# RWKV block-parallel chain: keys by token made by VectorE transposes and a DRAM exchange, and the spread of the block inverse four places down

## The reference, cut to what matters

```python
def rwkv7_scan(r, w, k, v, kk, a, s0):
    def step(s, inp):
        r_t, w_t, k_t, v_t, kk_t, a_t = inp
        s_kk = jnp.einsum('bhvk,bhk->bhv', s, kk_t)
        s = (s * w_t[:, :, None, :] - s_kk[..., None] * (kk_t * a_t)[:, :, None, :]
             + v_t[..., None] * k_t[:, :, None, :])
        return s, jnp.einsum('bhvk,bhk->bhv', s, r_t)
...
    for d, f in enumerate((_ident, _flip)):
        yc_d, s_ctx = rwkv7_scan(f(rc), f(wc), f(kc), f(vc), f(kkc), f(ac), s0)
        yl_d, _ = rwkv7_scan(f(rl), f(wl), f(kl), f(vl), f(kkl), f(al), s_ctx)
```

## Time and profile before

| | |
|---|---|
| median of three runs | 3613.45 us |
| the profiled execution, its own time | 3610.41 us |
| its span | 3608.6 us |
| granted TensorE clock, mean | 0.988 |
| chain of layer 0, first grams to last inverse store | 254.5 to 608.6 us |
| chain of layer 3, likewise | 2970.7 to 3297.3 us |

### The profile page before, as it was taken

One profiled execution on the slowest core, in us unless ns is written; L12 is line 12 of the kernel. 1 busy time (PEld: TensorE's weight loads), 2 busy tenths in 40 slices (PEclk: granted clock), 3 DMA queues, 4 the chain that ended last, 5 costly groups with the idle time before them and its releaser, 6 DMA issues. The chain is left out here.

```text
span 3608.6 us, 74335 instructions
## 1 busy us (share of the span) xinstructions
PE 3447.1 (96%) x28653; PEld 2513.5 (70%) x28653; DVE 2487.9 (69%) x4562; ACT 1156.4 (32%) x2482; POOL 590.4 (16%) x1128
## 2 busy tenths in 40 slices
PE   7998998999999999999999999999999997888999
PEld 2447777688786455555888876678877456777887
DVE  7986665489897657653898954469987956664431
ACT  4035554133202444431233014323310225663210
POOL 1015553000000323320000000000000105553000
PEclk9998999999999999999999999999999998999999
DMA  6641111244353323223444520043434541111454
GB/s 219 207 136 24 21 22 32 74 133 130 118 161 97 105 79 102 82 76 99 129 126 127 162 83 28 25 126 121 136 118 129 170 129 25 25 24 27 134 152 133
DMA packets 584315, 365.07 MB, mean 101 GB/s; under 512 B 126144, under 2 KB 553480, under 8 KB 581928
## 3 DMA queue, kind: packets, MB, share of 16 engines
q1 hardware_dynamic: 557544, 250.40, 25.1%
q0 software_dynamic: 26432, 110.07, 8.7%
HBM read 348.73 MB, written 11.67 MB: 100 GB/s over the span
## 5 line engine op out<-in xcount | busy, mean ns | idle before, releaser
L275 PE MATMUL PS<-H,WR 128*128 128x512 f32 (+1 forms) x1424 | 477.1, 494 | 0.0
L591 DVE SCALAR_TENSOR_TENSOR WORK<-WORK,SC 128x512 f32<-128x512 f32 x616 | 418.3, 746 | 0.7
L275 PEld LDWEIGHTS PS<-H,WR 128*128 128x128 f32 x1424 | 268.0, 190 | 187.3 <-issue 167.2
L2549 PE MATMUL PS<-WORK 64*64 64x64 f32 (+2 forms) x6944 | 361.0, 231 | 29.5 <-ACT BIG L2846 16.6
L571 POOL DMA_DIRECT2D WORK<-in_ada_w_dram x88 | 66.4, 755 | 1857.7 <-DVE WORK L591 839.6
L1474 PE MATMUL PS<-BIG,WR 128*128 128x512 f32 (+1 forms) x944 | 329.4, 503 | 5.2 <-DMA WR<-in_rw_wo_dram 1.7
L2549 PEld LDWEIGHTS PS<-WORK 64*64 64x64 f32 (+1 forms) x6944 | 282.1, 139 | 69.2 <-ACT WORK L2835 23.0
L1474 PEld LDWEIGHTS PS<-BIG,WR 128*128 128x128 f32 x944 | 175.7, 190 | 132.6 <-issue 111.8
L2835 ACT ACTIVATE WORK<-PS 128x64 f32<-128x64 f32 (+3 forms) x528 | 161.4, 326 | 292.0 <-PE PS L2549 286.7
L1012 ACT ACTIVATE WORK<-PS 128x512 f32<-128x512 f32 x252 | 134.7, 541 | 335.6 <-PE PS L945 285.1
L945 PE MATMUL PS<-BIG 128*128 128x256 f32 x984 | 223.9, 380 | 0.0
(11 more groups left out here) (363 smaller groups left out, 6391.0 us busy)
## 6 DMA issues: line engine op xcount, KB each, us to landing
WORK<-in_ada_w_dram POOLq DMA_DIRECT2D x88, 1024.0 KB, 6.3
WR<-in_ffn_w_in_dram SPq DMA_DIRECT2D x220, 256.0 KB, 2.9
BIG<-in_ffn_w_in_dram SPq DMA_DIRECT2D x132, 256.0 KB, 3.4
WR<-in_ffn_w_out_dram SPq DMA_DIRECT2D x106, 256.0 KB, 2.8
WR<-in_ssd_w_in_dram SPq DMA_DIRECT2D x96, 256.0 KB, 2.8
BIG<-scratch_dram POOLq DMA_DIRECT2D x8, 2048.0 KB, 7.9
BIG<-in_ffn_w_out_dram SPq DMA_DIRECT2D x36, 256.0 KB, 3.2
BIG<-in_ada_w_dram SPq DMA_DIRECT2D x4, 2048.0 KB, 15.5
```

The costliest lines, as they stand in the source:

```text
L275: mm = pe.matmul(outs, WR[:, slot, k, 0:m], rhs(k), start=first and k == 0, stop=last and k == nk - 1)
L591: lag(vec.scalar_tensor_tensor(ACC3[:, s_], w, by, ACC3[:, s_], ALU.mult, ALU.add), label)
L2549: return pe.matmul(o, lhs, rhs, start=start, stop=stop)
```

## The change

- `by_token` goes from TensorE and ScalarE (no HB steps) to VectorE as step TB. Per (i, s) there are four transposes of 128x256: of the replacement keys SD (n=1) for d = 0 and 1, then of the removal keys ADS (n=0) for both. VectorE's transpose turns 32x32 blocks within groups of 32 partitions, so the two blocks off the diagonal of each 64x64 land in the wrong partition group.
- BK has the same size and a new layout: [half, direction, which keys, a, 128], where a tells the 32 channels' column block; the four chunks of a half are interleaved, four elements apart. The block a = 1 - b % 2 of each partition group b is exchanged with its neighbour through a DRAM tensor `swapped`: `swap_out`, four DMAs of 32 partitions, a wait, `swap_in`, four DMAs. Each partition has four pieces of 128 elements in one of these.
- SyncE takes the swap of (i-1, 1) between `blocks_in(i, 0)` and `inverse_out(i, 0)`, that of (i, 0) between `blocks_in(i, 1)` and `inverse_out(i, 1)`, and the last one ahead of the output weights.
- `chain_s` waits for the swap at chunks 0 and 4 and takes its weights from BK with a step of four elements.
- TB stands at places 0 to 3 of slot (i, 0) and 0, 1, 4, 6 of slot (i, 1), after the chain's step. E moves from place 1 (s=0) or 2 (s=1) to 5; the levels Z and X from 4 to 14 (s=0) and 5 to 16 (s=1) to 8 to 18. Tile 0's half 0 keeps its places.
- The waits on HB fall away: `vt` for PSUM bank 7; `replacement` on ScalarE now waits for the key grams and for the transposes of the keys.

```diff
@@ -189,6 +189,8 @@
         scratch_stored = sem("scratch_stored")
         first_loaded = sem("first_loaded")
         gram_stored = sem("gram_stored")
+        swap_stored = sem("swap_stored")
+        swap_loaded = sem("swap_loaded")
         blocks_loaded = sem("blocks_loaded")
         inverse_stored = sem("inverse_stored")
         inverse_loaded = sem("inverse_loaded")
@@ -2342,7 +2344,8 @@
         RESET, KF, KK, BS = (work(T) for _ in range(4))
         INV = work(2 * T).rearrange("p (d c f) -> p d c f", d=2, c=NQ)
         TURN = work(T).rearrange("p (d c f) -> p d c f", d=2, c=4)
-        G2, BK, G1R = by_chunk(P), by_chunk(P), by_chunk(Q)
+        G2, G1R = by_chunk(P), by_chunk(Q)
+        BK = work(2 * NQ * P).rearrange("p (s d n a f) -> p s d n a f", s=2, d=2, n=2, a=2)
         sub = lambda: work(4 * Q).rearrange("p (c f) -> p c f", c=4)
         NSALL = work(16 * Q).rearrange("p (s d c f) -> p s d c f", s=2, d=2, c=4)
         NS = [[NSALL[:, s_, d] for s_ in range(2)] for d in range(2)]
@@ -2401,11 +2404,11 @@
             levels = [(k, q, s, m) for m in range(len(LEVELS)) for k in "ZX" for q in both]
             early, late = [], []
             if s == 0:
-                at = (4, 5, 7, 8, 10, 11, 13, 14) if i else (21, 21, 22, 22, 23, 23, 24, 24)
+                at = (8, 9, 11, 12, 14, 15, 17, 18) if i else (21, 21, 22, 22, 23, 23, 24, 24)
                 early += [(k, *step) for k, step in zip(at, levels)]
-                early += [(1 if i else 20, "E", i, 0), (0, "R", i, 0, 0), (2, "R", i, 0, 1), (9, "H2", both[0], 0),
-                          (12, "HB", both[0], 0, 0), (15, "HB", both[0], 0, 1), (16, "H2", both[1], 0),
-                          (18, "HB", both[1], 0, 0), (20, "HB", both[1], 0, 1)]
+                early += [(5 if i else 20, "E", i, 0), (0, "R", i, 0, 0), (2, "R", i, 0, 1), (9, "H2", both[0], 0),
+                          (16, "H2", both[1], 0)]
+                late += [(k, "TB", i, 0, d, n) for k, (d, n) in zip((0, 1, 2, 3), ((0, 1), (1, 1), (0, 0), (1, 0)))]
                 late.append((3, "Rv", i, 0))
                 if i == 0:
                     early += [(0, "IB0", 0, 0), (0, "IB", 0, 1), (0, "kf", 1), (0, "TS", 1)]
@@ -2417,11 +2420,11 @@
                         (5, "sum1"), (6, "KS"), (7, "KE"), (8, "pn0"), (9, "pr0"), (9, "pn1"), (11, "rm0"), (12, "ax0"),
                         (13, "ax1"), (14, "ar0"), (15, "ad0"))]
             else:
-                at = (5, 6, 8, 9, 12, 13, 15, 16)
+                at = (8, 9, 11, 12, 14, 15, 17, 18)
                 early += [(k, *step) for k, step in zip(at, levels)]
-                early += [(2, "E", i, 1), (14, "R", i, 1, 0), (17, "R", i, 1, 1), (2, "H2", both[0], 1),
-                          (3, "HB", both[0], 1, 0), (4, "HB", both[0], 1, 1), (7, "H2", both[1], 1),
-                          (10, "HB", both[1], 1, 0), (11, "HB", both[1], 1, 1)]
+                early += [(5, "E", i, 1), (14, "R", i, 1, 0), (17, "R", i, 1, 1), (2, "H2", both[0], 1),
+                          (7, "H2", both[1], 1)]
+                late += [(k, "TB", i, 1, d, n) for k, (d, n) in zip((0, 1, 4, 6), ((0, 1), (1, 1), (0, 0), (1, 0)))]
                 late.append((18, "Rv", i, 1))
                 if more:
                     early += [(d, "GT", i + 1, 0, d) for d in range(2)] + [(19 + d, "GT", i + 1, 1, d) for d in range(2)]
@@ -2487,7 +2490,7 @@
                         sp.dma_start(dst, src).then_inc(
                             side_loaded[3], C.mark(side_loaded[3], f"{t}.low" if dst is G2A else None, 16))
             parts_sp(f"mo{l}", a["rw_wo"][j], [(m, 0) for m in range(2)])
-            wide, narrow = blocks_dram
+            wide, narrow, swapped = blocks_dram
 
             def grams_out(i, s_):
                 for d in range(2):
@@ -2523,19 +2526,42 @@
                              narrow[s_ * size:s_ * size + size].rearrange("(x t j) -> t x j", x=8, j=BLK)).then_inc(
                     inverse_loaded, C.mark(inverse_loaded, f"{t}.t{i}.inverse{s_}", 16))
 
+            swap = swapped.rearrange("(s b p d n f) -> s b p d n f", s=2, b=4, p=32, d=2, n=2)
+
+            def swap_out(i, s_):
+                sp.wait_ge(vec_done, C.at(f"{t}.t{i}.tb{s_}"))
+                if i:
+                    sp.wait_ge(swap_loaded, C.at(f"{t}.t{i - 1}.bk{s_}"))
+                for b in range(4):
+                    sp.dma_start(swap[s_, b ^ 1], BK[32 * b:32 * b + 32, s_, :, :, 1 - b % 2, :]).then_inc(
+                        swap_stored, C.mark(swap_stored, f"{t}.t{i}.swap{s_}" if b == 3 else None, 16))
+
+            def swap_in(i, s_):
+                sp.wait_ge(swap_stored, C.at(f"{t}.t{i}.swap{s_}"))
+                for b in range(4):
+                    sp.dma_start(BK[32 * b:32 * b + 32, s_, :, :, 1 - b % 2, :], swap[s_, b]).then_inc(
+                        swap_loaded, C.mark(swap_loaded, f"{t}.t{i}.bk{s_}" if b == 3 else None, 16))
+
             for i in range(KD):
                 grams_out(i, 0)
                 blocks_in(i, 0)
                 if i == 0:
                     grams_out(i, 1)
                     blocks_in(i, 1)
+                else:
+                    swap_out(i - 1, 1)
+                    swap_in(i - 1, 1)
                 inverse_out(i, 0)
                 inverse_in(i, 0)
                 if i:
                     grams_out(i, 1)
                     blocks_in(i, 1)
+                swap_out(i, 0)
+                swap_in(i, 0)
                 inverse_out(i, 1)
                 inverse_in(i, 1)
+            swap_out(KD - 1, 1)
+            swap_in(KD - 1, 1)
             sp.wait_ge(vec_done, C.at(f"{t}.t{KD - 1}.sd1"))
             for m in (2, 3):
                 sp.dma_start(OUT_W[m], rows(a["rw_wo"][j])[:, :, m * P:(m + 1) * P]).then_inc(
@@ -2560,7 +2586,7 @@
                 done(mm(PS[:, 6, :], const("blk"), KK), f"t{n}.kks")
 
             def vt(n):
-                pe.wait_ge(act_done, C.at(f"{t}.{2 * n - 1}.bk1") if n else C.at(f"{t}.t{n}.a1"))
+                pe.wait_ge(act_done, C.at(f"{t}.t{n}.a1"))
                 for ch in range(NQ):
                     for hs in HALF:
 
@@ -2632,27 +2658,6 @@
                             last = mm(PS[hs, 6, c * P:c * P + P], SD[hs, d, cs], ar[hs, d, :, cs])
                 done(last, f"{q}.h2{s}")
 
-            def by_token(q, s, part_):
-                i, d = q // 2, q % 2
-                if part_:
-                    pass
-                elif d:
-                    pe.wait_ge(act_done, C.at(f"{t}.{q - 1}.bk{s}"))
-                elif s:
-                    pe.wait_ge(act_done, C.at(f"{t}.{q + 1}.bk0"))
-                elif i + 1 < KD:
-                    pe.wait_ge(act_done, C.at(f"{t}.t{i + 1}.a1"))
-                else:
-                    pe.wait_ge(act_done, C.at(f"{t}.t{i}.vt"))
-                for c in (2 * part_, 2 * part_ + 1):
-                    cs = tok(ORDER_Q[d][4 * s + c])
-                    for n, src in enumerate((ADS[i % 2], SD)):
-                        for hs in HALF:
-                            o = slice(c * P + n * Q, c * P + n * Q + Q)
-                            last = mm(PS[hs, 7, o], src[hs, d, cs], half_const("id64")[hs, :])
-                if part_:
-                    done(last, f"{q}.hb{s}")
-
             def z_step(q, s, m):
                 d, n = q % 2, LEVELS[m]
                 if m == 0:
@@ -2715,13 +2720,14 @@
                 ch = ORDER_Q[d][c]
                 v_tok, y = VTK[i % 2], PS[:, 2, tok(ch)]
                 if c % 4 == 0:
-                    pe.wait_ge(act_done, C.at(f"{t}.{q}.bk{c // 4}"))
+                    pe.wait_ge(swap_loaded, C.at(f"{t}.t{i}.bk{c // 4}"))
+                by_token = [BK[:, c // 4, d, n].rearrange("p a (f c) -> p (a f) c", c=4)[:, :, ch % 4] for n in range(2)]
                 pe.wait_ge(vec_done, C.at(f"{t}.{q}.us{c}"))
                 if c < NQ - 1:
                     for hs in HALF:
-                        mm(PS[hs, d, P:P + Q], BK[hs, d, c, Q:P], v_tok[hs, tok(ch)], stop=False)
+                        mm(PS[hs, d, P:P + Q], by_token[1][hs], v_tok[hs, tok(ch)], stop=False)
                     for hs in HALF:
-                        last = mm(PS[hs, d, P:P + Q], BK[hs, d, c, 0:Q], US[d][hs, :], start=False)
+                        last = mm(PS[hs, d, P:P + Q], by_token[0][hs], US[d][hs, :], start=False)
                     done(last, f"{q}.sp{c}")
                 if ch * Q < lo:
                     return
@@ -2814,7 +2820,7 @@
                             pe.wait_ge(side_loaded[3], C.at(f"{t}.low"))
                         stage_first(staging, u)
             pe.wait_ge(act_done, C.at(f"{t}.ve{KD - 1}"))
-            run({**staging, "GT": grams, "R": grams_r, "H2": grams_k, "HB": by_token, "Z": z_step, "X": x_step, "W": chain_w, "U": chain_u, "S": chain_s, "P2": post2, "P3": post3,
```

(25 more changed lines are left out.)

## The result

The changed kernel takes 3679.74 us (median of 4 runs, 3672.32 to 3681.95) against 3612.97 for the kernel before beside it: ratio 1.017, 95% interval 1.015 to 1.019. It is about 61 us slower by the ratio, and 90 us slower than forecast.

The account below looks back on a forecast made before the run. Dependence loops between tiles were taken as the bound: the chain in layer 0, SyncE and GpSimd in layer 3. Gains of 10.5, 4.7, and 5 and 3 (tails) sum to 23.2 us: 3590 us forecast, range 3575 to 3618.

Parts of the forecast that it names:

- Less 3.75 for the products: Chain's loop on TensorE, ScalarE and VectorE: removing 64 identity products takes 3.75 us of TensorE off each tile.
- 41.45: Layer 0 chain's loop per tile, in us, after taking 3.75 for products and 1.3 for VectorE's spread wait from 46.5.
- rival 5: The removed products only filled the chain's latency; the spread wait returns as one for the rates: 3613 us, chance 0.07.
- I take nothing: State products' weight loads with keys four elements apart: priced at nothing, upper bound 2.8 us a tile if doubled.
- Rival 2: No change or slower through strided weight loads in the state products: 3618 us if doubled, 3720 if four times; chance 0.11.
- 8 x 0.55 = 4.4: VectorE's eight added transposes of 128x256: 4.4 us a tile, bounds 3.6 and 8.0.
- three quarters on the path: Share of VectorE's added transpose time put on the chain's loop: 3.3 us a tile.
- I price the move at nothing elsewhere.: Moving spread and levels to later places removes VectorE's 3.2 us wait and TensorE's 1.9, and costs nothing elsewhere.
- The wait of L3158 for the DMA: Sign of the forecast: VectorE's 3.2 us wait for the spread inverse would be gone.
- Cost nothing: SyncE's eight DMAs and two waits per half tile, 7.3 us, fit where SyncE waits for the inverse: no cost.
- rival 3: SyncE is late with the inverse store if the swap takes over 12.5 us: some 3654 us, chance 0.05.
- rival 4: TensorE's granted clock falls after its new wait for the rates in layer 3: 12 us given back, 3602; chance 0.03.

Follow-up runs that it names:

- e1: The changed kernel with BK's axes reordered so that each chunk's 64 keys lie side by side: 3636.94 us, ratio 1.0065 to the kernel before.
- e5: Control: e1 with the state products loading 64x64 blocks of zeros in place of the keys; transposes, exchange and waits stay: 3636.17 us, ratio 1.0066.
- e7: e5 with each transpose replaced by a memset of one column of its output, same places and waits, exchange kept: 3618.97 us, ratio 1.001.
- e9: e7 with expand and spread in their old places and without the exchange, so the products' removal alone, memsets kept: 3619.02 us, ratio 1.0007.
- e13: e9 with the identity products issued again in their old places, not evicted and read by nobody: 3619.6 us, ratio 1.0006.
- e3: The kernel before with only the expand step and the spread moved to the changed kernel's places: 3627.0 us, ratio 1.0041.
- e4: The kernel before, identity products kept, with only the keys interleaved: ScalarE writes them four elements apart, state products load them so: 3633.15 us, ratio 1.0056.
- e2: The changed kernel with expand and spread back in their old places; transposes and exchange stay: 3671.15 us, ratio 1.0158 to the kernel before.
- e10: e1 with expand and spread back in their old places: 3632.64 us, ratio 1.0046 to the kernel before.
- e6: e5 without the exchange; the state products wait for the transposes instead of the last transfer in: 3633.6 us, ratio 1.0062.
- e11: e10 with the first half's transposes at places 0, 5, 6 and 6 in place of 0 to 3, SyncE's order kept: 3662.18 us, ratio 1.0122.

## Why the prediction was wrong

Forecast 3590, range 3575 to 3618, slower 0.16; measured 3680. The 61 us (by ratio) divide by the chain of runs: interleaving 38 us (changed kernel to e1), transposes 20 (e5 to e7, down to a memset), and 4 for all the rest together (e7 against before: the move, the exchange, the products and evictions gone, the memsets), not to be told from no change. The forecast failed in these steps.

**"Less 3.75 for the products."** This failed first. I subtracted the products' busy time from the chain's loop, as if TensorE were busy throughout the loop. e9 and e13 show that they are worth 0 and 0 us: e13 puts them back for nothing, so they run while TensorE would otherwise wait, and e9's waits name chain steps. So the tile stays at 46.5 us without the products too (46.8 in e9), and what was added afterwards had no room; my 41.45 had room for it that didn't exist. With the products at nothing the same sum gives 48.5 and 44.0 us a tile and some 3630 us in place of 3590, which is 40 of the 90 us missed. This was rival 5, at 0.07; its second half, late rates in place of a late spread, is near to what e3 shows. The rows allowed it: TensorE was idle 4.2 us of a tile, and the rows with waits of the earlier trace rows stand behind chain steps of VectorE. A loop with such waits is one of latencies, in which an engine's busy time is no term of its own. Asking where each of the eight parts stood, and what TensorE would wait for next without it, was the step left out.

**"I take nothing" for strided weight loads.** A mis-sized term: the doubled load of its upper bound was the truth (59 ns a record, 3.3 us a tile against the bound's 2.8). The row that I took as nearest, L608 with eight columns, is no strided weight load at all. Its weights in the kernel before:

```profile
L608 PEld LDWEIGHTS PS<-WORK x352: 132/138/138, 83.8 to 2968.8; 128*64 128x64 f32 x176
```

They are 64 columns side by side, loaded in 138 ns; the operand some elements apart is the moving one, of eight columns. The Trainium skill's rule on 16-byte lines (the page "Advanced Engine Details and Errata", SBUF Cachelines), by which accesses that touch a different line each time are penalised, is the one that I had quoted against the layout and then set aside. The runs agree with it: a load takes 0.135 us with keys side by side and 0.21 with keys four apart. Rival 2 named the mechanism and said 3618 for it, because it charged it against a gain that wasn't there. In the kernel before the interleaving costs 20 us, ScalarE's slower evictions included (e4). With transposes that write four apart it costs 38 (e1); no run parts the loads from the writes.

**"8 x 0.55 = 4.4", three quarters on the path.** A mis-sized term: they took 0.64 us, since they write four apart, within the bounds of 3.6 to 8.0. As 0.45 us transposes they cost 20 us (1.25 a tile) over memsets, less than the 3.3 a tile that I had put on the path. The head of slot s=0 is crowded, as said, but TensorE waits there for the state update without the transposes too (13.2 us in e3, 15.3 in e7, 16.5 in e1), so the share of that place in the 20 us is not shown.

**"I price the move at nothing elsewhere."** Wrong in the kernel before, 15 us (e3). Beside the transposes it is 4 to 7 us (e2, e10), at the edge of what can be told, and with neither products nor transposes nothing (e7 against e9). Behind these small totals stand 6 to 14 us lost in layer 0 each time. I had weighed the later grams of s=1 against a wait that goes; what came late was the chain's state update and, through ScalarE, the next tile's rates, as e3 shows, and these I hadn't looked at. The wait of L3158 for the DMA did go, as said, and paid nothing.

**"Cost nothing" for SyncE's exchange.** Right, shown by e6 for contiguous keys. The cover that I named is real, and so is the cost without it: transposes three or four places later let the store leave 3.65 us late and cost 27 us (e11), near rival 3's way of failing.

**The clock.** I had it as rival 4, 12 us at 0.03, from one idle of 1.94 us that did no harm. After 1.97 and then 1.20 us of idle the clock stood at the 1.2 GHz level until 492; the earlier trace rows showed a lower clock after 3.36. In layer 0 it takes 2.2 us of TensorE a tile, 1.8 in e1 and 0.8 in e7. It comes behind waits, and I can't say how much of the 61 us it carries, since no run held the clock fixed.

Open: what exactly holds the tile at 46.5 us when the products are gone. e9's waits point to VectorE's copy of U, behind other VectorE work, but no run shortened that step. Open too: why the new places help in layer 3 once the products are gone.

## What to carry to other kernels

Work removed from the busiest engine is worth nothing where it filled waits of a dependent chain; take it out alone, and then put it back as a dummy, before building what replaces it. Read a change stage by stage also when its total is small: here a loss in one layer stood against a gain in the other. Don't let a layout make a matmul's stationary operand strided: reordering the axes of the tile cost nothing and gave back more than half of the loss. When in-order queues carry a round trip, a new transfer has two deadlines, the consumer's and that of the transfer behind it, and moving its producer by a few places can miss the second.

## What the runs showed of the hardware

- A 64x64 fp32 weight load with columns four elements apart: 59 ns a record from start to start and about 0.21 us each; contiguous 29 ns and 0.135 us.
- A 128x256 fp32 transpose on VectorE that writes four elements apart: 643 ns, contiguous 446. ScalarE's copy of 128x512 from PSUM: 1.10 us four apart, 593 ns contiguous.
- The exchange through DRAM in pieces of 128 bytes, while it was hidden: no measurable time (e6).
